# A scan shared by four engines: products, scaling, squares and taps in another order, and the first blocks of a layer taken by k

## The reference

```python
def conformer_branch(u_glu, dw_w, dw_b, ln_g, ln_b, w_out):
    a, g = jnp.split(u_glu, 2, axis=-1)
    v = a * jax.nn.sigmoid(g)
    v = causal_dwconv(v, dw_w, dw_b)          # 31 taps, 1024 channels
    v = jax.nn.silu(layer_norm(v, ln_g, ln_b))
    return v @ w_out
...
# ssd_chunked: 4 groups of 8 heads, chunks of 128 positions, state 128
    xs = (x * dt[..., None]).reshape(b, c, L, g, r, p)
...
    cb = jnp.einsum("bclgn,bcsgn->bcgls", cc, bc)
    y_diag = jnp.einsum("bcgrls,bcsgrp->bclgrp", cb[:, :, :, None] * decay, xs)
    decay_states = jnp.exp(a_cs[..., -1:] - a_cs)
    states = jnp.einsum("bclgn,bcgrl,bclgrp->bcgrpn", bc, decay_states, xs)
    ... # prev: the states, carried from chunk to chunk
    y_off = jnp.einsum("bclgn,bcgrpn,bcgrl->bclgrp", cc, prev, jnp.exp(a_cs))
    return (y_diag + y_off).reshape(b, t, h, p)
...
# ssd_branch, behind it
    yg = (y.reshape(bsz, t, SSM_DIM) * jax.nn.silu(z.astype(jnp.float32)))
    yg = yg * lax.rsqrt(jnp.mean(jnp.square(yg), axis=-1, keepdims=True) + RMS_EPS)  # per group
    return yn @ w_out
```

## Time and profile before

| what | us |
|---|---|
| median of 3 runs | 2259.47 |
| the profiled execution | 2259.66 |
| its span in the trace | 2257.6 |
| TensorE busy | 2191.2 |
| VectorE busy | 1457.6 |
| ScalarE busy | 960.8 |
| GpSimd busy | 51.1 |
| scan, first `xdt` of group 1 to first of group 2 | 63.0 |
| `group_sums` starts | 429.3 |

### The profile page before, as it was taken

The page is one execution under the profiler, slowest core; times in us unless marked ns, Lnnn a source line. Parts: engine busy times, 40 slices in busy tenths (PEclk is TensorE's granted clock), DMA queues, the critical chain, the costliest instruction groups (busy, mean ns, idle before and its releaser), DMA issues.

```text
span 2257.6 us, 31794 instructions
## 1 busy us (share of the span) xinstructions
PE 2191.2 (97%) x12988; PEld 1916.5 (85%) x12988; DVE 1457.6 (65%) x1853; ACT 960.8 (43%) x1393; POOL 51.1 (2%) x33
## 2 busy tenths in 40 slices
PE   9999999999999999999999999999999999999997
PEld 6887777777787888878999999999998988888886
DVE  4878999899767566545776684235367668622544
ACT  5447565731535444433546443223233564422321
POOL 1000100100000000000200000000000000000000
PEclk9999999999999999999999999999999999999998
DMA  4223222322222222234221222222222112222221
GB/s 152 96 102 111 105 89 98 103 83 85 94 93 75 94 96 108 95 132 148 81 76 38 94 75 94 80 90 94 94 76 98 57 57 94 93 94 93 94 95 55
DMA packets 35696, 207.68 MB, mean 92 GB/s; under 512 B 4931, under 2 KB 6979, under 8 KB 12261
## 3 DMA queue, kind: packets, MB, share of 16 engines
q1 hardware_dynamic: 28944, 193.48, 24.2%
q10 hardware_dynamic: 6612, 12.23, 1.7%
HBM read 203.52 MB, written 2.17 MB: 91 GB/s over the span
## 4 chain that ended last, share of the span: by engine, by line
PE 78%; DVE 11%; DVEq 4%; ACT 3%; issue 1%; ACTq 1%; DMA 0%
PE PS L545 24%; PE PS L549 24%; PE PS L547 24%; DVE vout L2068 5%; DVEq L2061 2%; DVE wlo L1826 1%; PE PS L1063 1%; DVE hres L2009 1%; DVEq L2008 1%; PE PS L1037 1%; ACT whi L1168 1%; DVE zres L2007 0%; PE PS L1053 0%; DVE res L1950 0%; PE PS L632 0%
## 5 line engine op out<-in xcount | busy, mean ns | idle before, releaser
L545 PE MATMUL PS<-ahi,whi 128*128 128x512 f32 (+2 forms) x2368 | 730.6, 344 | 15.2 <-DVE wlo L1826 4.2
L547 PE MATMUL PS<-alo,whi 128*128 128x512 f32 (+2 forms) x2368 | 718.1, 338 | 0.0
L549 PE MATMUL PS<-ahi,wlo 128*128 128x512 f32 (+2 forms) x2368 | 717.1, 338 | 0.0
L1826 DVE TENSOR_TENSOR wlo<-raw,whi 128x2048 fp32r<-128x2048 f32 x172 | 393.9, 2291 | 455.0 <-ACT whi L1168 454.5
L1168 ACT ACTIVATE whi<-raw 128x2048 fp32r<-128x2048 f32 x168 | 321.6, 1914 | 671.7 <-PE PS L549 669.0
L545 PEld LDWEIGHTS PS<-ahi,whi 128*128 128x128 f32 x2368 | 413.4, 189 | 78.8 <-issue 25.0
L549 PEld LDWEIGHTS PS<-ahi,wlo 128*128 128x128 f32 x2368 | 412.4, 189 | 48.3
L547 PEld LDWEIGHTS PS<-alo,whi 128*128 128x128 f32 x2368 | 412.8, 189 | 47.5 <-issue 1.2
L545 PE MATMUL PS<-f2hi,whi 128*128 128x264 f32 (+2 forms) x800 | 214.9, 314 | 0.0
L547 PE MATMUL PS<-f2lo,whi 128*128 128x264 f32 (+2 forms) x800 | 214.8, 314 | 0.0
L549 PE MATMUL PS<-f2hi,wlo 128*128 128x264 f32 (+2 forms) x800 | 214.8, 314 | 0.0
(11 more groups left out here) (342 smaller groups left out, 2662.4 us busy)
## 6 DMA issues: line engine op xcount, KB each, us to landing
raw<-weights SPq DMA_DIRECT2D x180, 1024.0 KB, 4.7
acs_b<-acs_rows ACTq DMA_DIRECT2D x34, 256.0 KB, 3.3
const<-const ACTq DMA_DIRECT2D x2, 1232.0 KB, 5.6
x_in<-x_t SPq DMA_DIRECT2D x4, 512.0 KB, 6.1
out_t<-hres SPq DMA_DIRECT2D x16, 128.0 KB, 1.7
raw<-weights SPq DMA_DIRECT2D x1, 512.0 KB, 10.5
cols<-columns ACTq DMA_DIRECT2D x1, 385.0 KB, 7.4
const<-const ACTq DMA_DIRECT2D x1, 256.0 KB, 5.0
```

Source lines behind the costliest of these rows:

```text
L545: nc.tensor.matmul(o, wh, h, start=first, stop=False)
L547: nc.tensor.matmul(o, wh, h, start=False, stop=False)
L549: mm = nc.tensor.matmul(out[j], wl, hi[j], start=False, stop=last)
L1826: v.tensor_tensor(wlo[s][:, :], raw[s][:, :], whi[s][:, :].bitcast(F32), ALU.subtract).then_inc(lo_ready, 1)
```

## The change

All of it is a new order and new buffers; the arithmetic is the same.
- GpSimd's products start at a new semaphore `gate_go`, given by VectorE at the head of each `y_out` but the first (for the product of the tile before) and once ahead of `glu(1)`. The sixteenth product moves to VectorE.
- `x_scaled` for tiles 0 and 1 of the next group comes behind `glu(1)` of this one.
- The first state tile leaves PSUM on ScalarE (`st_copy`, behind `head(2)`), with VectorE waiting for it in `bt_ok`. The two operations ahead of the wait are masks 0 and 1, where `taps(0)` stood.
- Squares of group 0 and 1 are made in the group after, and added there at once; those of group 2 in the last group. Only the last group's stand behind the scan. The squares get buffers `y_squares(k)`.
- Tile 2's taps leave `late_tiles`: five in each of the groups 1 to 3, the rest in `ssm_out`. `TAPS_AT` and `LAST_TAPS` have new numbers; the last group runs through the same code as the others, so that 21 instead of 16 of tile 7's taps are done before `ssm_out`.
- `first_units` takes both units in a block for 5 of 8 k in the second half too.

```diff
-TAPS_AT = [0, 4, 5, 8, 9, 11, 13, 16, 31]
-LAST_TAPS = [9, 13, 16]
+TAPS_AT = [0, 4, 8, 9, 12, 14, 18, 26, 31]
+LAST_TAPS = 21
...
-            with pool.Fori(0, GROUPS) as g:
-                def gated(j):
-
-                    hold(pool, y_ok, g * GP + (j + 1), "pool")
-                    hold(pool, zs_ok, 2 * g + (j // 2 + 1), "pool")
...
+            for k in range(XT - 1):
+                pool.wait_ge(zs_ok, k // 2 + 1)
+                pool.wait_ge(gate_go, k + 1)
+                t = xbc[:, k * T:(k + 1) * T]
+                nc.gpsimd.tensor_tensor(t, t, zs[k % GP][:, :], ALU.mult).then_inc(yg_ok, 1)
...
-                    orders = [(k, (0, 1)) for k in range(KD)] if h == 0 and w[1] is not w2[stage.slot(1)] else [
-                        (k, (u,)) for u in range(2) for k in range(KD)]
+                    both = range(KD - 3 if h else KD if w[1] is not w2[stage.slot(1)] else 0)
+                    orders = [(k, (0, 1)) for k in both] + [(k, (u,)) for u in range(2) for k in range(len(both), KD)]
...
+                def st_copy():
+                    act.wait_ge(st_ps, g + 1)
+                    nc.scalar.activation(st[:, 0:T], bank(0), ACT.Copy).then_inc(bt_ok, 1)
+
...
+                if g in (1, 2):
+                    for k in range(GP * g - GP, GP * g - 1):
+                        y_square(k)
                 glu_unit(0)
-                head(0)
-                head(1)
-                if g < GROUPS - 1:
-                    head(2)
-                    head(3)
+                if g in (1, 2):
+                    y_square(GP * g - 1)
+                for q in range(3):
+                    head(q)
+                st_copy()
+                head(3)
                 z_unit(1)
...
+            def squares_added(g):
+
+                acc = sumsq[g][:, 0:T]
+                for j in range(1, GP):
+                    dve.wait_ge(ysq_ok, g * GP + j + 1)
...
                 def y_out(j):
 
                     hold(dve, y_mm, g * GH + 2 * (j + 1), "dve")
+                    if j:
+                        drain().then_inc(gate_go, 1)
...
+                    if g and n < 5:
+                        long_taps([2], 5 * (g - 1) + n, 5 * (g - 1) + n + 1)
+
+                if g in (1, 2):
+                    squares_added(g - 1)
+                mask(0)
+                mask(1)
+                dve.wait_ge(bt_ok, 2 * g + 2)
...
-                hold(dve, st_ps, g + 1, "dve")
-                v.tensor_copy(st[:, 0:T], bank(0))
...
                 if g < GROUPS - 1:
...
                     taps(6)
+                    low_next(stage, 2 * g + 1, 1)
+                    hold(dve, sig_ok, 2 * g + 3, "dve")
+                    drain().then_inc(gate_go, 1)
+                    glu(1)
+                    for j in range(2):
+                        x_scaled(g + 1, j)
                     taps(7)
```

More of the change, by code:

```diff
@@ L384, in build @@
                              "st_ok", "cbm_ok", "exp_ok", "mc_ok", "y_mm", "y_ok"))
+        gate_go = sem("gate_go")
         sig_ok, v_ok = sem("sig_ok"), sem("glu_used")
@@ L896, in _ @@
                 hold(pe, xds_ok, g + 1, "pe")
-                hold(pe, bt_ok, g + 1, "pe")
+                hold(pe, bt_ok, 2 * g + 1, "pe")
                 for c in range(CHUNKS - 1):
@@ L1470, in _ @@
             stage = WORK["gate_b"]
-            for k in range(GP, XT):
+            for k in range(XT - GP, XT):
                 y_square(k)
@@ L2150, in _, with x_scaled @@
             stage = WORK["z_glu"]
-            late_tiles = [u for u in range(2, KD, 2)]
+            late_tiles = [u for u in range(4, KD, 2)]
+            def squares_added(g):
+                acc = sumsq[g][:, 0:T]
+                for j in range(1, GP):
+                    dve.wait_ge(ysq_ok, g * GP + j + 1)
+                    if j > 1:
+                        drain()
+                    v.tensor_tensor(acc, y_squares(g * GP) if j == 1 else acc, y_squares(g * GP + j), ALU.add
+                                    ).then_inc(ysq_sum, 2 if j == 1 else 1)
+            xdt3 = xdt[:, :].rearrange("p (c n) -> p c n", c=CHUNKS)
+            def x_scaled(g, j):
+                dve.wait_ge(xt_ps, g * GP + (j + 1))
+                for hh in range(2):
+                    o = v.tensor_tensor(
+                        xdt3[:, :, j * P + hh * 64:j * P + (hh + 1) * 64],
+                        bank(j % 2).rearrange("p (c n) -> p c n", c=CHUNKS)[:, :, hh * 64:(hh + 1) * 64],
+                        tok[:, 128:256].rearrange("p (c h) -> p c h", c=CHUNKS)[:, :, bass.ds(g * GH + (2 * j + hh), 1)]
+                        .to_broadcast([P, CHUNKS, HEAD_P]), ALU.mult)
+                o.then_inc(xdt_ok, 1)
             for g in range(0, GROUPS):
@@ L2244, in gated_sums @@
-            def gated_sums(tiles):
-                for k in tiles:
-                    acc = sumsq[k // GP][:, 0:T]
-                    if k % GP:
-                        dve.wait_ge(ysq_ok, k + 1)
-                        if k % GP > 1:
-                            drain()
-                        v.tensor_tensor(acc, ysq4[0][:, :] if k % GP == 1 else acc, ysq4[k % 4][:, :], ALU.add
-                                        ).then_inc(ysq_sum, 2 if k % GP == 1 else 1)
-            mask(0)
-            mask(1)
@@ new lines, in _ @@
+                mask(3)
+                taps(0)
+                y_out(0)
+                taps(1)
+                low_next(stage, 2 * g, 1)
+                taps(2)
+                y_out(1)
+                mask(4)
+                mask(5)
+                taps(3)
+                if g == GROUPS - 1:
+                    squares_added(2)
+                y_out(2)
+                taps(4)
+                mask(6)
+                low_next(stage, 2 * g + 1, 0)
+                mask(7)
+                taps(5)
@@ new lines, in _ @@
+                y_out(3)
+                if g < GROUPS - 1:
+                    taps(6)
+                    low_next(stage, 2 * g + 1, 1)
[4 more added lines that the diff above has]
+                        x_scaled(g + 1, j)
+                    taps(7)
+            last = xbc[:, (XT - 1) * T:XT * T]
+            dve.wait_ge(zs_ok, 2 * GROUPS)
+            dve.wait_ge(yg_ok, XT - 1)
@@ L2274, in _ @@
+            drain()
+            v.tensor_tensor(last, last, zs[GP - 1][:, :], ALU.mult).then_inc(yg_ok, 1)
+            squares_added(GROUPS - 1)
             for s in range(2):
```

106 lines of the change are left out of this document (30 added, 76 removed).

## The result

Over 20 runs of each kernel, the changed one has a median of 2264.8 us and the one before 2258.1. The ratio is 1.0030, with a 95% interval of 1.0023 to 1.0036: slower by 6.7 us. The range of the prediction (2248 to 2270) holds the time. The point (2260.5) is 4.3 us too low, and the likeliest case (within 0.2%) did not come: the time is nearest to that of the rival "slower, 2266". The profiled execution took 2266.0 us (span 2264.0), 6.4 more than that of the kernel before, and what follows accounts for these 6.4.

A forecast was written before the change was run, and what follows sets the result against it. The prediction took VectorE as the scan's bound, with slack on TensorE. Terms: scan +16.4, behind it -1.6, ssm_out -6.3, borders -7.5, together +1.0 on 2259.7; 2260.5 us against the median, range 2248 to 2270.

The forecast's parts named there:

- the likeliest case: Whole kernel: time within 0.2% of before, spanning 2256 to 2265 us; chance 0.40, together with the rival of missed product slots.
- slower, 2266: Scan: TensorE's new waits each bring a clock drop, VectorE idles longer at the copy; total 2266 us, chance 0.31.
- The bound of the scan: Scan: VectorE is the bound, busy 57.6 of 63 us in one group; TensorE has slack; sum for the scan +16.4 us.
- The products: Scan: 12 at the head of a y_out cost VectorE 0.38 us each plus drain, 1.5 a group, for 3.9 before.
- The rival in which the products miss their slots: Scan: each group's third product runs beside taps, +0.5 us each, +2; total 2263, its chance counted in the forecast's 0.40.
- The taps: Extra taps at 0.82 us each: +4.0 us in groups 1 and 2 each, +8.2 in the last; ssm_out -6.3.
- The copy of st: Scan: VectorE saves 0.77 us a group but idles 6.8 in group 0, about 2 in groups 1 and 2, 3.8 last.
- Behind the scan: From the group sums to 478 us TensorE is the bound; its wait of 1.64 us at 466.20 goes: -1.6.
- The borders: Blocks by k in the second half of borders: waits go, 3.2, 2.8 and 1.5 us won, -7.5 in all.
- x scaled early: Scan: removes TensorE's 9.3 us of waits at the xdt transposes, but wins nothing as long as VectorE is the bound.
- The last stretch of the scan: Last group: mask 7 at 431.8 us, then TensorE's work plus 1.7 for a clock drop, group sums at 445.7.
- The squares: Scan: a sum costs VectorE 0.77 us; +2.3 in groups 1 and 2 each, -4.1 in the last group.

The follow-up runs named there:

- e4: The changed kernel without the extra taps in the scan (tile 2's all in ssm_out, last group 16 of tile 7's): 2257.0 us, ratio to before 0.9994.
- e7: The changed kernel with GpSimd's products released by y_ok as before instead of by gate_go: 2278.3 us, ratio to before 1.0085.
- e11: e9 with the extra taps in the scan, in the changed kernel's places: 2248.8 us, ratio to before 0.9968.
- e6: The kernel before with only GpSimd's products timed by gate_go, none moved to VectorE: 2257.4 us, ratio to before 0.9999.
- e9: e5 with mask(7) ahead of the third low part on VectorE and head(7) ahead of its high part on ScalarE: 2242.2 us, ratio to before 0.9931.
- e2: The changed kernel with ScalarE's copy of st moved ahead of head(2), behind head(1): 2257.4 us, ratio to before 1.0002.
- e5: The changed kernel with the edits of both e2 and e4: 2249.0 us, ratio to before 0.9957.
- e8: The changed kernel with x tiles 0 and 1 scaled at the start of their own group again: 2268.3 us, ratio to before 1.0045.
- e1: The kernel before with the edit of first_units alone (both units in a block for 5 of 8 k): 2250.8 us, ratio to before 0.9962.
- e10: e9 with four taps of tile 7 of the last group moved behind the last squares: 2242.6 us, ratio to before 0.9938.
- e3: The changed kernel with the copy of st on VectorE again, behind masks 0 and 1: 2258.5 us, ratio to before 1.0000.

## Why the prediction was right, and where not

The total was forecast 5.4 us too low for the profiled execution (+1.0 for +6.4): 1.4 in the scan, 1.6 behind it, 2.7 elsewhere, less 0.3 that `ssm_out` and the borders gave beyond their terms. That the scan is within 1.4 us is in part luck, as the terms below miss in both directions.

- **The bound of the scan** was read right from the earlier trace rows: e4, e7 and e11 move VectorE's work by 15 to 16 us and the scan follows by 12.5 to 18. It was read too sharply, though. e6 took 3 to 4 us a group from VectorE and the groups became 2.6 us shorter, and e9 took nothing from it and one of them became 3.3 us shorter.
- **The products** were mis-sized. From the earlier trace rows a product at the head of a `y_out` was put at 0.38 us; it costs 0, the sum behind it stays at 0.56 everywhere (the forecast's sign was 0.9). The row had a product that began 0.05 us into the second PSUM operation; those that begin with the first have 1.29 us of PSUM reads beside them. Some 1.1 us a group too much, on the slow side. The rival in which the products miss their slots did not come: each of the 15 starts at its `gate_go`.
- **The taps**: 16.2 us in the sum, 12.5 (e11) and 14.3 to 17.9 (e4) on the chip, and **-6.3** in `ssm_out` against 6.5 measured. This term is right, though the parts given for it (5.7 and 1.7, less 1.8) add up to 5.6.
- **The copy of st**: 6.8 us of VectorE's idling in group 0 forecast, 0.57 + 2.28 + 4.04 = 6.9 measured; in groups 1 and 2 "about 2", measured 1.4 and 5.2; in the last 3.8, measured 0.9 + 3.6. The step that failed is the 5.2: the sum had let head(2) start with no wait for its row in the middle groups, and in the third group the row came 3.1 us late; the other 2.1 are the "about 2". The periods forecast at 66.6 us each are 65.0 and 68.8, 1.6 too long and 2.2 too short.
- **Behind the scan** the step "its wait of 1.64 at 466.20 goes: -1.6" failed. The wait is there, of the same length, at 484.00, 36.87 us behind the group sums where it was 36.88 behind them before. It is 36.9 us in e2, e4, e5 and e8 to e11 as well, with the taps in the scan or out of it: the way to it starts at the group sums (root, scales, y, the low part between them), and earlier or fewer taps have no part in it.
- **The borders** were right in all three places, within 0.2 us each, and e1 shows that the whole reaches the end.
- **x scaled early** was put at nothing; e8 says 2 to 3 us of gain.
- **The last stretch of the scan.** VectorE's side came out within a microsecond, by misses that cancel: mask 7 was forecast at 431.8, and TensorE goes on at `pair(3)` at 432.07. From there to the group sums 13.9 us were forecast and 15.1 measured, and that is most of the 1.4. The term that was mis-sized is the clock drop, 1.7 in the sum: the clock was at half for some 7 us, which is over 3 lost. The stretch in the changed kernel, and in e4, which has the same work there at full clock (granted clock in the third column from the right):

```profile
432.07:447.13 15.06, 15.06 (x64) 12.00 (x64) 10.56 (x14) 4.67 (x5) 1.29 (x1) 0.79 0.21 71
```

```profile
417.04:429.19 12.15, 12.15 (x65) 9.79 (x65) 9.07 (x12) 7.11 (x10) 1.30 (x1) 1.00 0.32 108
```

- **The clock.** The rival "slower" said that new waits would each be followed by half clock. Of the ten waits of the changed kernel in the scan, seven were, those of 2.15 us and more; the three of 0.79, 1.05 and 1.29 us were not. The length alone does not decide it: in e5 a wait of 2.48 us was followed by half clock and one of 2.54 was not. The granted clock in the four stretches of the changed kernel is 0.97, 0.95, 0.93 and 0.89. Both of that rival's conditions came true (3.76 us at a `pair(3)`, 5.23 us at the copy), and its time, 2266, is the nearest of all. Its way to the longer idling, a later end of `z_glu(0,1)`, is not what the rows of the 5.23 us show: 3.09 of them are the DMA row. And in the groups ahead of the last `pair(3)` half clock need not cost anything: e10 has none in the scan and e9 has two stretches of it, and their group sums are 0.4 us apart. Behind the last `pair(3)`, where TensorE sets the pace, it counts, 2.9 us against e4. How much of the rest of the 17.8 us is clock was not separated further.
- **The squares** were not tried alone, and what they are worth is not shown.

The Trainium skill (GPSIMD Engine Reference, Key points) says that VectorE is about twice as fast for elementwise work. The trace agrees: the sixteenth product takes 0.69 us on VectorE, the others 1.27 to 1.30 on GpSimd. All of them on VectorE was not tried; since a well placed product on GpSimd costs VectorE nothing, as above, VectorE would by these rows have 0.77 us more to do for each.

## What to carry to other kernels

When an operation moves to an engine with idle time, look at what stands ahead of it in that engine's queue: here a copy of 0.6 us behind a head that waits for a DMA row cost the kernel 7 us, and one place earlier it was no worse than on the engine it came from. When TensorE waits for the last of several small operations, look for a long one that is not yet needed among them: moving a 2.3 us weight split behind a 0.7 us mask, and ScalarE's part of the split behind its head, gave 6 to 7 us. Work that is moved between two stages that are both bound by the engine that does it need not win anything; here the taps cost one stage twice what the other gave back.

## What the runs showed of the hardware that was not expected

GpSimd's products of 1.27 to 1.31 us cost VectorE nothing beside operations that read PSUM. Beside work with two operands in SBUF a product cost VectorE 0.9 to 1.1 us in e7 and was longer itself (1.47 to 1.85): five taps took 4.91 us for 4.05, two masks 2.35 for 1.29, and the low part of a weight 3.38 for 2.29:

```profile
296.95 3.38 DVE L1831 TENSOR_TENSOR wlo<-raw,whi 128x2048 fp32r<-128x2048 f32 x1
```

The late row of head(2) stands beside a unit of weights in the same trace. ScalarE asks for the row and the sync engine for 1 MB of weights at nearly the same time; from 324 to 328 us the DMA engines are busy at 0.84 (the column before the last) and the row lands just before 327.8, 6 us after it was asked for. In the group before, the weights were asked for at 256.89, and the row asked for at 255.65 was there by 259.0:

```profile
321.77 0.36 ACTq L1408 DMA_DIRECT2D acs_b<-acs_rows  x1
...
321.87 0.33 SPq L478 DMA_DIRECT2D raw<-weights  x1
...
324.00:328.00 4.00, 4.00 (x17) 2.98 (x16) 2.01 (x4) 0.89 (x3) 0.00 (x0) 1.00 0.84 327
```

The same stands once in each of e2, e3, e4, e5, e7 and e8: a row asked for 0.1 us ahead of such weights is used 6.0 to 6.2 us after it was asked for, where the median from asking to landing is 3.3 in the changed kernel. In e6 it is the row of the last group (6.5 us). In e2 and e5 the copy no longer stands behind the row. That the weights delay the row is read from these places; it was not tried with the weights moved.
